# Where two of the four weight sums of each mixed tile are made: VectorE, or two loads and two accumulating DMAs

## The reference, cut to what matters

```
y = silu(rms_norm(h) @ w_gate) * (rms_norm(h) @ w_up)      # 1024 -> 2816, twice
h = h + 0.5 * (y @ w_down)
```

## Time and profile before

| | |
|---|---|
| median of 3 runs | 1890.58 us (1890.55 to 1890.62) |
| the profiled execution | 1890.69 us, its span 1888.9 us |
| PE busy | 1860.7 us (99% of the span) |
| DVE busy | 1357.9 us (72%) |
| ACT busy | 890.9 us (47%) |
| POOL busy | 261.4 us (14%) |
| L491, the instruction that the change removes | 68 times, 82.8 us in all |
| HBM read | 175.04 MB, 94 GB/s over the span |
| granted TensorE clock | 0.9 or more in every one of 40 slices; mean 0.997 |

### The profile page before, as it was taken

The page is one execution under the profiler, slowest core; times in us unless marked ns, Lnnn a source line. Parts: engine busy times, 40 slices in busy tenths (PEclk is TensorE's granted clock), DMA queues, the critical chain, the costliest instruction groups (busy, mean ns, idle before and its releaser), DMA issues.

```text
span 1888.9 us, 31440 instructions
## 1 busy us (share of the span) xinstructions
PE 1860.7 (99%) x11418; PEld 1617.9 (86%) x11418; DVE 1357.9 (72%) x1981; ACT 890.9 (47%) x1503; POOL 261.4 (14%) x204
## 2 busy tenths in 40 slices
PE   8999999999999999999999999999989999999998
PEld 6899988777799998887899998877657899998886
DVE  8788788774988874357888864279984988874355
ACT  7355542245555554224455553134573655554222
POOL 0000001212200000225000001073243100000225
PEclk9999999999999999999999999999999999999999
DMA  5232333333233333323333343332101333333321
GB/s 179 90 109 94 109 98 108 93 100 89 75 99 100 111 105 118 103 76 99 102 89 101 111 123 90 99 109 67 57 1 46 91 100 100 111 103 119 102 77 56
DMA packets 56753, 179.88 MB, mean 95 GB/s; under 512 B 12144, under 2 KB 12144, under 8 KB 56656
## 3 DMA queue, kind: packets, MB, share of 16 engines
q1 hardware_dynamic: 54656, 173.69, 29.9%
q0 software_dynamic: 928, 3.02, 0.5%
q10 hardware_dynamic: 1088, 2.10, 0.3%
HBM read 175.04 MB, written 3.15 MB: 94 GB/s over the span
## 4 chain that ended last, share of the span: by engine, by line
PE 88%; DVE 7%; ACT 2%; POOL 1%; issue 1%; DMA 0%; DVEq 0%; SPq 0%; POOLq 0%; ACTq 0%
PE ps L2288 36%; PE ps L2250 26%; PE ps L2232 18%; PE ps L2736 2%; PE ps L2399 1%; DVE sm L1265 1%; PE ps L2635 1%; DVE work L1241 1%; DVE w_lo L384 1%; POOL sumsq L1541 1%; DVE stat L1239 1%; DVE x_lo L436 1%; ACT prob L1970 0%; PE ps L2654 0%; PE ps L2450 0%
## 5 line engine op out<-in xcount | busy, mean ns | idle before, releaser
L384 DVE TENSOR_TENSOR w_lo<-raw,w_hi 128x1024 fp32r<-128x1024 f32 x174 | 231.9, 1341 | 217.1 <-ACT w_hi L376 215.8
L376 ACT ACTIVATE w_hi<-raw 128x1024 fp32r<-128x1024 f32 x186 | 194.1, 1054 | 300.0 <-PE ps L2250 248.7
L2288 PE MATMUL ps<-xs_hi,w_hi 128*128 128x256 f32 x1088 | 308.4, 283 | 0.5
L2288 PE MATMUL ps<-xs_lo,w_hi 128*128 128x256 f32 x1088 | 308.1, 283 | 0.0
L2288 PE MATMUL ps<-xs_hi,w_lo 128*128 128x256 f32 x1088 | 308.0, 283 | 0.0
L2250 PE MATMUL ps<-act_hi,w_hi 128*128 (+1 forms) x720 | 280.6, 390 | 0.0
L2250 PE MATMUL ps<-act_lo,w_hi 128*128 (+1 forms) x720 | 280.3, 389 | 0.0
L2250 PE MATMUL ps<-act_hi,w_lo 128*128 (+1 forms) x720 | 280.2, 389 | 0.0
L2232 PE MATMUL ps<-x_hi,w_hi 128*128 128x512 f32 x640 | 258.1, 403 | 8.9 <-ACT w_hi L376 7.6
L2232 PE MATMUL ps<-x_hi,w_lo 128*128 128x512 f32 x640 | 250.7, 392 | 0.0
L2232 PE MATMUL ps<-x_lo,w_hi 128*128 128x512 f32 x640 | 250.6, 392 | 0.0
(11 more groups left out here) (406 smaller groups left out, 3547.5 us busy)
## 6 DMA issues: line engine op xcount, KB each, us to landing
raw<-in_weights SPq DMA_DIRECT2D x322, 512.0 KB, 3.6
h<-in_xT ACTq DMA_DIRECT2D x4, 512.0 KB, 6.8
out<-result SPq DMA_DIRECT2D x4, 512.0 KB, 3.0
p_raw<-in_pT POOLq DMA_DIRECT2D x2, 512.0 KB, 4.0
scratch_u<-u_sc SPq DMA_DIRECT2D x1, 512.0 KB, 5.9
u_grp<-scratch_u SPq DMA_DIRECT2D x1, 512.0 KB, 4.3
scratch_y<-y_grp SPq DMA_DIRECT2D x2, 256.0 KB, 3.0
y_ch<-scratch_y SPq DMA_DIRECT2D x1, 512.0 KB, 3.5
```

What stands on the lines that cost most here:

```text
L376: act.activation(w_hi[:, slot], raw[:, slot], ACT.Copy).then_inc(hi_ready, 1)
L384: dve.tensor_tensor(w_lo[:, slot], raw[:, slot], w_hi[:, slot].bitcast(F32), SUB)\
L2288: last = pe.matmul(ps[:, bank, 0:HALF], w[:, at, cols], x[:, k], start=(start and k == 0 and part == 0), stop=(stop and k == KH - 1 and pa ...
```

## The change

The sums `w_sum[0]` and `w_sum[1]` are no longer written by DVE. For each mixed tile POOL issues two plain loads of 256 KB (128 rows of 2 KB) from the weights in HBM, waits for both, and issues two accumulating DMAs of 256 KB, each of which adds the block own 2 (again from HBM) to what lies in SBUF. The two sums have two buffers: `w_sum[:, 0:2]` for the even tiles of a pair, `other_sums` (over rows 0 and 1 of `x_lo`) for the odd ones. POOL starts on a tile when the tile two before it has been split (`t_ready`) and summed (`w_sums`). For the first mixed tile it starts as soon as the norm's `rstd` is there, for the second when PE has done the last plain tile (`chunk_used`). DVE still makes the third and fourth sum, in two instructions, after a wait for `blocks_added`; ACT waits for `blocks_added` ahead of the high parts of T1 and T3. L491 is gone. The call of `block_sums` stands in POOL's queue ahead of `s5_loads`, `load_embedding`, `sum_squares(pool, 5)` and `load_embedding`, for f = 0 to 3.

```diff
+        other_sums = over("other_sums", [P, 2, T], at_x_lo)
...
+        def loaded_sums(b):
+            return other_sums[:] if b % 2 else w_sum[:, 0:2]
...
                 for k in range(2):
                     dve.wait_ge(raw_loaded[slot + k], turn_of(first, 2 * b + k, i) * 16 + 16)
-                dve.tensor_tensor(w_sum[:, 0:2], own[:, 0:4:3],
-                                  own[:, 2].unsqueeze(1).to_broadcast([P, 2, T]), ADD)\
+                dve.wait_ge(fast["blocks_added"], 32 * counted(1, f, i, b, 1))
+                dve.tensor_tensor(w_sum[:, 2], loaded_sums(b)[:, 0], own[:, 3], ADD)\
                    .then_inc(fast["w_sums"], 1)
-                dve.wait_ge(fast["w_sums"], counted(3, f, i, b, 1))
-                dve.tensor_tensor(w_sum[:, 2], w_sum[:, 0], own[:, 3], ADD)\
-                   .then_inc(fast["w_sums"], 1)
-                dve.wait_ge(fast["w_sums"], counted(3, f, i, b, 2))
+                dve.wait_ge(fast["w_sums"], counted(2, f, i, b, 1))
                 dve.tensor_tensor(w_sum[:, 3], w_sum[:, 2], own[:, 1], ADD)\
                    .then_inc(fast["w_sums"], 1)
...
+        def block_sums(pool, f, first):
+            plain = PLAINS[f]
+            pair = plain // 2
+            def sums(i, b, opening=False):
+                dst = loaded_sums(b)
+                if opening:
+                    if b:
+                        pool.wait_ge(chunk_used, first + 2 * plain)
+                else:
+                    pool.wait_ge(fast["t_ready"], counted(2, f, i, b - 2, 2))
+                    pool.wait_ge(fast["w_sums"], counted(2, f, i, b - 2, 1))
+                gate, up = (A["weights"][bass.ds(i * 4 + (first + 2 * b + k), 1)]
+                            .rearrange("a p b f -> (a p) (b f)") for k in range(2))
+                pool.dma_start(dst[:, 0], gate[:, 0:T]).then_inc(fast["blocks_loaded"], 16)
+                pool.dma_start(dst[:, 1], up[:, T:]).then_inc(fast["blocks_loaded"], 16)
+                pool.wait_ge(fast["blocks_loaded"], 32 * counted(1, f, i, b, 1))
+                pool.dma_start(dst[:, 0], up[:, 0:T], accum_op=ADD).then_inc(fast["blocks_added"], 16)
+                pool.dma_start(dst[:, 1], up[:, 0:T], accum_op=ADD).then_inc(fast["blocks_added"], 16)
+            sums(pair, 0, opening=True)
+            sums(pair, 1, opening=True)
+            with pool.Fori(pair + 1, NF // 2, 1) as i:
+                sums(i, 0)
+                sums(i, 1)
...
             def sums_hi(i, b, which):
...
-                act.wait_ge(fast["w_sums"], counted(3, f, i, b, (3, 1)[which]))
+                if which == 0:
+                    act.wait_ge(fast["w_sums"], counted(2, f, i, b, 2))
+                else:
+                    act.wait_ge(fast["blocks_added"], 32 * counted(1, f, i, b, 1))
```

More of the change, by code:

```diff
@@ L327, in encoder @@
         fast = {n: sem(f"fast_{n}") for n in (
+            "blocks_loaded", "blocks_added",
             "x_gained", "x_normed", "x_sums", "x_hi", "x_ready", "w_sums", "t_hi",
@@ L502, in sums_lo @@
                 at = halves_of(first, b)[("T24", "T13")[which]]
-                src = w_sum[:, 2:4] if which == 0 else w_sum[:, 0:2]
+                src = w_sum[:, 2:4] if which == 0 else loaded_sums(b)
                 turned = isinstance(i, int) and 2 * i + b < plain + 2
@@ L1628, in _ @@
                 .then_inc(const_ready, 1)
+            pool.wait_ge(rstd_ready, 1)
+            block_sums(pool, 0, STARTS[0])
             s5_loads(pool)
@@ L1634, in _ @@
             sum_squares(pool, 2)
+            pool.wait_ge(rstd_ready, 3)
+            block_sums(pool, 1, STARTS[3])
             load_embedding(pool, 0, 3)
@@ L1637, in _ @@
             sum_squares(pool, 4)
+            pool.wait_ge(rstd_ready, 5)
+            block_sums(pool, 2, STARTS[5])
             sum_squares(pool, 5)
@@ L1640, in _ @@
             sum_squares(pool, 6)
+            pool.wait_ge(rstd_ready, 7)
+            block_sums(pool, 3, STARTS[8])
             load_embedding(pool, 1, 8)
```

## The result

The changed kernel takes 1999.88 us (median of 4 runs, 1992.04 to 2000.71), the kernel before 1890.6 us beside it: ratio 1.0569, 95% interval 1.0555 to 1.0583. That is 109 us slower, where 10.8 were forecast and 1940 us was the end of the range. The profiled execution took 2000.51 us, its span 1998.8 us.

What follows compares the result with a forecast made beforehand. TensorE, busy 1860.7 of 1888.9 us, was taken as the bound. Gain 0, steady tiles 0 and openings 4 x (10.0 - 7.3) = 10.8 us on 1890.69 gave 1901.5, so 1901.4 us against the median; range 1890 to 1940 us.

Steps and rivals of the forecast that it cites:

- What L is: Step pricing a mixed tile's four transfers: 8.2 + 0.2 + 1.6 = 10.0 us, from 7.3 to 13.5 us.
- L: Time in a mixed tile from when GpSimd may start until both loaded sums are there; forecast 10.0 us.
- SP's chunks: Term for SP's 512 KB loads: one falling into the mixed tile's transfer window adds 0 to 2.0 us.
- The second read: Term for an accumulating pair also reading its 512 KB of target in mixed tiles: 0 to 2.0 us.
- The budgets: Time allowed from GpSimd's start to the sums: 13.5 us in steady mixed tiles, 7.3 us in each block's second.
- the law beyond them: Each us over 13.5 costs half a us per steady tile; each over 7.3 costs one us, four times.
- the steady rival: Slow adder or GpSimd held up by VectorE: some 60 steady tiles lose (L - 13.5) / 2 each; chance 0.22.
- What goes away: L491 removed from VectorE in mixed tiles, 82.8 us beside TensorE's work: gain 0.
- The openings: Second mixed tile of each of four blocks: TensorE idle some 2.7 us each, 10.8 us in all; chance 0.58.
- hidden: Third mixed tile of a block: sums 5.3 us after the second's, wanted 7.3 us after, so no cost.
- SP's chunks: covered: In mixed tiles SP's loads land in 3.6 us, wanted 13.3 us later; a doubled landing time costs nothing.

Runs made afterwards that it cites:

- Plain pairs: The changed kernel with accum_op left out of the second pair, so all four transfers are plain and each sum lacks an addend: 1905.93 us.
- one sum: The changed kernel with half of the transfers, one load and one addition per tile; VectorE makes the second sum: 1903.41 us.
- four buffers: The changed kernel with the loaded sums in four buffers instead of two, the first two tiles of each block filled early: 1891.37 us.
- the openings without transfers: The changed kernel, but VectorE makes the first two sums of the second mixed tile of each block: 1968.89 us.
- One addition for two: The changed kernel with a tile's two additions issued as one transfer of 512 KB that reads the same block for both targets: 1980.97 us.
- The copy experiment: The changed kernel with ScalarE's fourth copy into part_sum ahead of the high parts of T2 and T4: 2013.47 us.
- the probe: The kernel before with six 256 KB transfers added on GpSimd's queue late in the program, plain and accumulating, single and paired: 1890.73 us.
- thin chunks: The changed kernel, but SP's looped loads bring only the first 512 bytes of each row, 64 KB in place of 512: 1913.84 us.

## Why the prediction was wrong

**The step that failed is "What L is".** 10.0 us were taken, at most 13.5; in the steady tiles L is 16.3 us. In the tile shown, from 93.18: the loads are there at 101.2, 8.0 us (forecast 4.1 and a hand-over); the additions 9.1 us later (forecast 4.1 + 1.6). The prices with little beside the chain were nearly right: 10.8 us for 10.0, with about 4.1 us for the pair of loads, as forecast. What failed were the bounds of two terms. SP's chunks, bounded by 2.0 us for one of them, are worth 4.8 us in the loop. The second read, bounded by 2.0 us from the difference of two plain loads, is worth 4.3 us there: a pair of additions takes 8.0 us from its first issue on, where a plain pair in its place takes 4.6, and the loads beside it take 6.9 us instead of 6.0. (With little beside it the pair of additions takes 6.3 us, 2.2 more than plain.) The landings behind these bounds were of single transfers in other stages, and L is two pairs in a row beside SP's chunks. The two shares overlap and are not a sum, but it takes both to lose time in the steady tiles: without the accumulating kind L is 12.0 us, without SP's chunks 11.5, each under 13.5.

**The budgets and the law beyond them held.** With the measured L the steady rival's formula gives 60 x (16.3 - 13.5) / 2 = 84 us, and the openings 4 x (11.2 - 7.3) = 16 us: 100 of the measured 109. It was the rival "the steady tiles are late too", with "about 2000" at L = 16, and a chance of 0.22. Of its two causes, a slow adder is half of it, and GpSimd held up by VectorE was not seen. Plain pairs (12.0 us: no steady loss), one sum (10.4 us: none; 5.7 us forecast by the budget for its openings, 6.3 measured), four buffers and the openings without transfers (78 us) lie on the same law. One addition for two has 90 us, where the formula gives 51 + 17; there what follows L is 7.0 us in the mean, not 6.7, which explains some 9 of the other 22.

**What goes away: 0.** Right; four buffers show it.

**The openings.** Releaser and place were right, 4.1 us each instead of 2.7. Two things were missing. One is the clock behind each stop, some 1.5 to 3 us. The other, on the scale of the earlier trace rows, is the third tile. GpSimd issued its loads 5.26 us after the opening's, forecast 5.3, but the sums came at 97.18, 9.5 us after the second tile's, where "hidden" had allowed 7.3. Little came of it: TensorE's next stop is one of 0.3 us, at 101.11.

**Behind the wait.** The prediction named only what VectorE has queued behind L498. ScalarE's high parts of T2 and T4 wait too, and its fourth copy stands behind them, for which TensorE's last product of the current tile waits. That is where the 57.1 us of stops appear; the forecast would have looked for them at L517. The copy experiment shows that the place changes, not the loss.

**The remaining 9 us.** They belong to the openings, since without the openings' transfers nothing remains beside the formula. The clock behind the four stops is worth about as much (9.6 us, the estimate above); that it is the cause is not shown. In the steady tiles the slower clock adds nothing to the formula: L and the 6.7 us behind it make 23.0 us, and two tiles took 22.95 us in the mean.

**SP's chunks: covered.** Right: `raw` lands in 4.1 us instead of 3.6, and nobody waits for it.

**The rules weighed.** VectorE keeps nothing from GpSimd that could be seen: its issues take 0.57 and 0.89 to 1.22 us in the loop beside a busy VectorE (the two of 1.03 and 0.96 us at 81.83 and 82.45 came while VectorE stood waiting), 0.54 and 0.87 to 1.17 us in the probe. With plain pairs beside the same VectorE all four take 0.54 us, so the longer issue belongs to the accumulating kind. So the port rule of SBUF — State Buffer in the Trainium skill (SBUF: two separate sides) plays no part in this loss. A lone addition took 4.2 us where a lone load took 2.7, 1.5 us more. The two source reads that Collectives: The Full Stack of the Trainium skill gives a reducing transfer (The bandwidth ceiling: the fold count and why AG ≠ RS ≠ AR) would make it 1.0 more for 256 KB by the forecast's rate, so the trace agrees in direction, and the measured surcharge is half as large again.

**Not tried:** three buffers, a version that starts the loads by the release of the single half-buffers, and a run that tells whether SP's chunks hold the transfers up in the DMA engines or in the memory behind them. No version was faster than the kernel before; four buffers only draw level.

## What to carry to other kernels

A step that is taken off an engine with time to spare and put on a queue wins nothing and becomes a latency: count it against the time between the release of its buffer and its use (here 13.5 us at two buffers), and if it doesn't fit, add buffers before you make it faster. Price such a chain beside the traffic that it will run with, not by single landings elsewhere in a profile: here 15.5 us from the first issue against 10.8. And list what stands behind the wait on every engine that waits, not only on the first.

## What was not expected of the hardware

- Dependent transfers beside SP's chunks: a 256 KB load from 2.7 us alone to 6.0 us (second of a pair, issued at 94.54), an addition from 4.2 to 8.6 us (issued at 101.77), at a DMA share of 0.67. Another engine's queue doesn't help (5.8 us). Beside thin chunks the loads are back at 3.0 and 3.3 us in the mean, although the DMA share is still 0.55.
- An accumulating transfer costs its issuer more: 0.87 to 1.22 us against 0.54 to 0.59.
- A stop of TensorE of 2.8 us is followed by a granted clock of 0.66 over the next 4 us, and costs some 1.5 us more than itself. So do stops of 1.8 and 2.0 us in the same run, but not one of 1.9 us, nor the first one of 3.3 us with thin chunks (clock 1.00 over the next 4 us).
- A single accumulating transfer can read one block for two targets. It takes 6.9 us in the mean where the pair takes 8.0 us from the first issue.
